# Attention probabilities transposed by a matmul with a diagonal that holds their factor

## What is computed

```python
def _masked_softmax(s, mask):
    ...
    p = jnp.where(mask, jnp.exp(s - m), 0.0)
    return p / jnp.maximum(jnp.sum(p, axis=-1, keepdims=True), 1e-30)
...
o_dsa = jnp.einsum('bhqk,bqkd->bqhd', p.astype(vg.dtype), vg)
...
o_nsa = o_cmp * gt[..., 0:1] + o_slc * gt[..., 1:2] + o_win * gt[..., 2:3]
...
p = jax.nn.softmax(s, axis=-1).astype(v.dtype)          # memory attention
o = jnp.einsum('bhqm,bmhd->bqhd', p, v)
```

## Time and profile before

| | |
|---|---|
| profiled execution | 2762.7 us, its span 2760.9 us |
| median of three runs | 2763.45 us |
| PE busy | 2534.0 us (92%) |
| DVE, ACT, POOL busy | 1292.1, 1049.2, 1250.8 us |
| mean granted clock of PE | 0.95 |
| attention of block 2, units2 | about 2034 to 2264 us of the span |
| memory attention | about 2340 to 2379 us |

### The profile page before, as it was taken

One profiled execution on the slowest core, in us unless ns is written; L12 is line 12 of the kernel. 1 busy time (PEld: TensorE's weight loads), 2 busy tenths in 40 slices (PEclk: granted clock), 3 DMA queues, 4 the chain that ended last, 5 costly groups with the idle time before them and its releaser, 6 DMA issues.

```text
span 2760.9 us, 33141 instructions
## 1 busy us (share of the span) xinstructions
PE 2534.0 (92%) x12115; PEld 2020.5 (73%) x12115; DVE 1292.1 (47%) x2515; ACT 1049.2 (38%) x1619; POOL 1250.8 (45%) x1638
## 2 busy tenths in 40 slices
PE   4898989999999999898999999988886899899998
PEld 3686767888888788676788878877654457688887
DVE  7785442453435577534343251344578853622111
ACT  4233663332222433465242222252255564533322
POOL 4243434656656644334565555562232234355554
PEclk9899999999999999999999999998888589999999
DMA  3221222332222322122233222231110002123222
GB/s 129 70 76 55 71 69 73 104 108 99 92 100 90 106 73 74 58 73 69 81 111 110 98 88 97 91 131 66 50 47 1 1 1 69 58 95 99 92 99 84
DMA packets 80145, 218.05 MB, mean 79 GB/s; under 512 B 15728, under 2 KB 25328, under 8 KB 79472
## 3 DMA queue, kind: packets, MB, share of 16 engines
q1 hardware_dynamic: 60912, 200.96, 22.3%
q10 hardware_dynamic: 19072, 14.98, 1.9%
HBM read 207.25 MB, written 2.10 MB: 76 GB/s over the span
## 4 chain that ended last, share of the span: by engine, by line
PE 76%; DVE 18%; ACT 3%; issue 2%; ACTq 1%; DMA 0%; POOL 0%; DVEq 0%
PE psG L864 22%; PE psG L865 22%; PE psG L866 22%; DVE work_m L1712 3%; DVE tmp L1712 2%; PE psO L1038 1%; DVE work_b L1712 1%; DVE b_lo L1712 1%; DVE work_b L2122 1%; PE psO L1104 1%; DVE max L2121 1%; DVE work_m L1933 1%; PE psT L1015 1%; DVE work_b L2006 1%; PE psG L1049 1%
## 5 line engine op out<-in xcount | busy, mean ns | idle before, releaser
L807 POOL TENSOR_TENSOR w_lo<-w_raw,w_hi 128x256 fp32r<-128x256 f32 x1494 | 1167.8, 813 | 1313.5 <-ACT w_hi L1292 1313.3
L864 PE MATMUL psG<-h_hi,w_hi 128*128 128x512 f32 x1880 | 757.8, 403 | 34.6 <-POOL w_lo L807 30.8
L865 PE MATMUL psG<-h_lo,w_hi 128*128 128x512 f32 x1880 | 740.3, 394 | 0.0
L866 PE MATMUL psG<-h_hi,w_lo 128*128 128x512 f32 x1880 | 739.1, 393 | 0.0
L1292 ACT ACTIVATE w_hi<-w_raw 128x1024 fp32r<-128x1024 f32 (+4 forms) x417 | 403.5, 969 | 497.5 <-PE psG L866 481.2
L864 PEld LDWEIGHTS psG<-h_hi,w_hi 128*128 128x128 f32 x1880 | 358.4, 191 | 122.6 <-issue 43.4
L865 PEld LDWEIGHTS psG<-h_lo,w_hi 128*128 128x128 f32 x1880 | 358.7, 191 | 76.3 <-issue 4.5
L866 PEld LDWEIGHTS psG<-h_hi,w_lo 128*128 128x128 f32 x1880 | 357.9, 190 | 76.8
L864 PE MATMUL psG<-m_hi,w_hi 128*128 128x512 f32 x800 | 311.6, 389 | 1.5 <-DVE m_lo L1712 1.5
L866 PE MATMUL psG<-m_hi,w_lo 128*128 128x512 f32 x800 | 311.2, 389 | 0.0
L865 PE MATMUL psG<-m_lo,w_hi 128*128 128x512 f32 x800 | 311.2, 389 | 0.0
(11 more groups left out here) (284 smaller groups left out, 2940.2 us busy)
## 6 DMA issues: line engine op xcount, KB each, us to landing
w_raw<-wstream SPq DMA_DIRECT2D x327, 512.0 KB, 3.3
w_raw<-wstream SPq DMA_DIRECT2D x64, 256.0 KB, 2.6
w_raw<-wstream SPq DMA_DIRECT2D x16, 384.0 KB, 3.0
work_b<-work_b ACTq DMA_DIRECT2D x16, 256.0 KB, 3.8
work_b<-cmpw ACTq DMA_DIRECT2D x2, 2048.0 KB, 7.7
x<-xT SPq DMA_DIRECT2D x4, 512.0 KB, 6.2
small_work<-ssmp ACTq DMA_DIRECT2D x8, 256.0 KB, 4.1
outT<-x SPq DMA_DIRECT2D x1, 2048.0 KB, 6.3
```

The source lines that it names most:

```text
L807: ins = pool.tensor_tensor(lo[:, c], w[:, c], hi[:, c].bitcast(F32), ALU.subtract)
L864: pe.matmul(out, whi, hi, start=(k == 0), stop=False)
L865: pe.matmul(out, whi, lo, start=False, stop=False)
L866: ins = pe.matmul(out, wlo, hi, start=False, stop=(k == K - 1))
```

## The change

Scaling p is left out. Instead the 128x128 identity is multiplied by the same factor of each row into a new buffer, a diagonal matrix for each a (`factors`, four buffers in turn), by POOL for `units2` and by DVE for x. The blocks of p are turned by an ordinary fp32 matmul with p as the stationary operand and that diagonal as the moving one, in place of a transpose with the identity. POOL and DVE get a wait for the transposes of four units earlier, whose diagonal they overwrite. sw units keep scaling and transpose.

```diff
+        def factors(u):
+
+            return work(R2, 11264 + 256 * (u["n"] % 4), [P, 2, P])
...
             def scale_probs(u):
 
                 n = u["n"]
-                p, _ = probs(u)
-                st = stats(u)
+                st, diag = stats(u), factors(u)
                 pool.wait_ge(s_norm, n - units2[0]["n"] + 1)
+                if n - units2[0]["n"] >= 4:
+                    pool.wait_ge(s_tr, n - 3)
...
-                    ins = pool.tensor_scalar(p[:, a], p[:, a], st[:, 8 + a:9 + a], gate, ALU.mult, ALU.mult)
+                    ins = pool.tensor_scalar(diag[:, a], ident, st[:, 8 + a:9 + a], gate, ALU.mult, ALU.mult)
...
                     for i, m in key_blocks(u):
-                        ins = pe.transpose(out[0:m, a, i * P:(i + 1) * P], p[:, a, i * P:i * P + m], ident)
+                        o, block = out[0:m, a, i * P:(i + 1) * P], p[:, a, i * P:i * P + m]
+                        if u["kind"] == "sw":
+                            ins = pe.transpose(o, block, ident)
+                        else:
+                            ins = pe.matmul(o, block, factors(u)[:, a], start=True, stop=True)
...
-                    ts(p[:, 0], p[:, 0], st[:, 8:9], None, ALU.mult)
-                    ts(p[:, 1], p[:, 1], st[:, 9:10], None, ALU.mult, None, s_prob)
+                    if kind == "x" and n - units["x"][0]["n"] >= 4:
+                        dve.wait_ge(s_tr, n - 3)
+                    out, src = (factors(u), (ident, ident)) if kind == "x" else (p, (p[:, 0], p[:, 1]))
+                    ts(out[:, 0], src[0], st[:, 8:9], None, ALU.mult)
+                    ts(out[:, 1], src[1], st[:, 9:10], None, ALU.mult, None, s_prob)
```

## The result

The changed kernel takes 2773.89 us, the median of five runs (2771.54 to 2780.25); the kernel before took 2763.45 us in five runs beside it (2760.20 to 2767.26). The ratio is 1.0036, 95% interval 1.0024 to 1.0049: slower by some 10 us. The forecast was 2780, with a range of 2764 to 2789. The profiled execution of the changed kernel took 2772.92 us with a span of 2771.1 us.

What follows compares the result with a forecast made beforehand. PE was taken to bound several attention stretches, DVE or ACT the others. Stretch terms summed to +19.6 us, less 3 for the clock, +16.6 on 2762.7, 2779.3 us, stated as 2780; range 2764 to 2789.

Steps and rivals of the forecast that it cites:

- The price of a block: PE, each turned block: a second instruction costing what the first costs, 0.11 us at the full clock, 0.22 at the half.
- 2041 to 2061: First NSA units beside the indexer, PE without pause: 26 more block instructions, +3.4 us.
- The rival of four transposes: All turned blocks: each costs four times a transpose, total about 2832 us; chance 3%.
- 2106 to 2120: Stretch taken as PE without pause: 16 blocks at the full clock, less 0.3 us of pauses, +1.5 us.
- 2152 to 2174: PE without pause at the half clock: 16 blocks, +3.5 us; a clock rise over half the stretch gives 3 back.
- the first rival: Full clock returns in both PE-bound stretches, -10.5 and -8 us, total 2764.6, no measurable difference; chance 14%.
- 2203 to 2223: Narrow NSA units of b = 0, PE without pause: 18 blocks at 0.22 us, nothing hides them, +4.0 us.
- DSA: DSA units, two halves of 42 blocks each: +4.0 us where PE leads, +2.7 where ACT leads and covers part.
- The stretches that DVE leads: Where DVE's selection covers PE: 112 blocks, some 15 us on PE, of which +1.0 us is seen.
- the rival in which it fails: DVE-led stretches: the selection no longer covers PE, half of 15 us is seen, total 2789.5; chance 13%.
- POOL and its new wait: POOL: shorter instructions give nothing more, and the new wait for earlier transposes costs nothing.
- Memory attention: After units2: shorter DVE scalings -1.0 us, bounds -1.5, transposes ahead of a value product +0.5; together -0.5 us.

Runs made afterwards that it cites:

- e5_b1_only: Kernel before, with the change only for the twelve NSA units of query block b = 1: 2766.55 us against 2767.02, ratio 0.9996.
- e2_twice: Kernel before, with each transpose of units2 and memory attention issued twice, scaling of p kept: 2766.74 us, ratio 1.0017.
- e1_null: Kernel before run again without any edit, to see the scatter of profiles: 2767.02 us in one run, beside 2765.22 us in 29 runs.
- e7_fill_b12: Kernel before, plus one unused 512-column fp32 matmul in each unit of b = 2 and b = 1 without an indexer head: 2765.73 us, ratio 0.9994.
- e10_change_b210: Kernel before, with the change only for the NSA units of query blocks b = 2, 1 and 0: 2761.47 us against 2765.35, ratio 0.9987.
- e4_no_dsa: The change without the DSA units, which keep scaling on POOL and the transpose: 2766.10 us, ratio 1.0007 to the kernel before.
- e3_memory_only: Kernel before, with the change for memory attention alone: 2764.56 us, ratio 1.0000.
- e9_twice_nsa: Kernel before, with transposes of the NSA units of all four query blocks issued twice, the others once: 2766.94 us, ratio 1.0002.
- e11_twice_b210: Kernel before, with the transposes of the NSA units of b = 2, 1 and 0 issued twice: 2762.19 us, ratio 0.9988.

## Why the prediction was right, and where not

The direction and the mechanism were right: one more instruction for each of 304 blocks, paid where PE leads. Point by point:

- **The price of a block**, 0.11 us at the full clock: right. Measured (2.05 - 1.09) / 8 = 0.12 us, and 608 instructions of 275 ns. At the half clock e5_b1_only shows +3.3 us for units 24 to 28, where the working had +3.5. The rival of four transposes is out.
- **2041 to 2061**, +3.4 us: measured +3.0, in e2_twice too.
- **2106 to 2120**, +1.5 us: measured -1.1. The working took 0.3 us of pauses where the earlier trace rows show 1.76 (12.24 busy of 14), so it misread a stretch with room as one without. The added work went into the pauses: PE was busy for 15.33 of 18.20 us in units 12 to 16 before and for 16.40 of 17.10 after. The clock rose too (0.91 to 1.00), and this group moved by -0.7 us without any change (e1_null); no run separates the three.
- **2152 to 2174**, +3.5 and -3 for the clock: the rise that was thought likely came, but for the whole of the four units, not for half of them, and it is worth 7.9 us. It is the largest miss of the sum, 5 us. The step that failed is "half of the stretch at the full clock": the clock was already full as unit 24 began and stayed so, and what raised it was work in b = 2 (e7_fill_b12, e10_change_b210), not that of the stretch itself (e5_b1_only). For this stretch the first rival came true, with a smaller gain than its price: 15 us in place of 22 would have been 7 us less than before, and it is 4.6.
- **2203 to 2223**, +4.0 us: measured +3.8 in the change and in e4_no_dsa. The first rival wanted a full clock here too; it was 0.52. That it stayed low was assumed, not derived: e2_twice, with as many instructions, was 8.1 us shorter here. The clock of the change's other executions (0.956 to 0.957) gives no sign that they differ from the profiled one.
- **DSA**, +4.0 and +2.7, together 6.7 us: measured 7.3, of which e4_no_dsa shows 6.6 to be the diagonal's. Right, in size and in the reason: PE leads to the end of the DSA units (busy for 23.63 of the last 25.00 us), and the second half (+3.2) costs a little more than thought. The working has no term for what follows: behind DSA the change gains 2.5 us on e4_no_dsa (column 63-64).
- **The stretches that DVE leads**, +1.0 us: 0.3 - 0.9 + 0.2, nothing that can be told from the scatter. The cover held; the rival in which it fails is out.
- **POOL and its new wait**, nothing: right. The profile puts one pause of POOL, 2.9 us before 2237.84, down to L1024. But the diagonal to be overwritten there was that of unit 46, turned from 2228.3 on, long before; what ended just ahead of 2237.84 is the reciprocal of its own unit (L2037, 2237.58 for 0.17 us). The unit was turned at 2239.57, so it held nobody up.
- **Memory attention**, -0.5 us: measured -2.5, and +2.2 behind it. The net, -0.3, is about what was said, but by luck, for a reason that the working didn't have: the clock was 1.00 there in place of 0.75, and fell just behind. e3_memory_only shows both by itself, and a time unchanged. Up to 1.0 us of the 2.5 is scatter (e1_null).

The working added 16.6 us. By the table 6.6 us were paid from unit 0 to the end, and by the ratio 10 us. Units 24 to 28 (-4.6 for +0.5) and 12 to 16 (-1.1 for +1.5) are 7.7 us of the 10 us between the working and the table, the end of DSA and the products behind it 1.1 (the column 63-64), and DVE's stretches 1.4. The first, 5.1 us, is the clock by e5_b1_only, and most of why the forecast was 6 us too high: the clock's term was sized for half of one stretch. In units 12 to 16 and behind DSA the clock was higher too (0.91 to 1.00, 0.94 to 0.96), but no run takes it out there.

What stays open: what decides the clock of units 37 to 46 (0.52, 0.86, 0.59, 0.53 and 0.54 in five kernels, two of which give PE the same instructions), why e2_twice had a higher mean clock than the change in most of its executions, so whether the kind of instruction has a part in that, and whether the fall behind memory attention is tied to a full clock within it. It stood so in the change, e3_memory_only, e4_no_dsa and e2_twice; but e7_fill_b12 and e9_twice_nsa lost over 4 us there with the code of memory attention unchanged, and e11_twice_b210 nothing.

## What to carry to other kernels

Folding a factor into a transposition by a matmul with a diagonal saves work on the engine that scaled, and costs PE an fp32 matmul's second instruction for each block: do it only where PE has pauses in the same stretch, and not where PE is next to lead, as in DSA here. Cost it by stretch, and give the clock an account of its own, with a term for the whole of a stretch and not for half (7.9 us of 21.9 here), since work added in one stretch can raise the clock of the next. Before a change of the clock is put down to an edit, look at two executions of the kernel without it. A gain from the clock in one part isn't a gain in the time until the runs show it: in e3, e7, e9 and e10 the rest of the kernel was 2.3 to 4.2 us longer.

## What the runs showed of the hardware

- With doubled transposes the clock rose in units 24 to 28 as with matmuls (e2_twice and the change, 1.00 in place of 0.50, -4.6 us in both), and so it did with matmuls that computed nothing, in units ahead of them (e7_fill_b12, -5.1 us). Once, with doubled transposes in e11_twice_b210, it did not (0.66).
- A higher clock did not always buy time: units 24 to 28 of the same kernel took 18.6 us at 0.50 and 18.5 us at 0.66 (before, e1_null).
- More PE work made the next stretch shorter: sixteen fp32 matmul instructions added to units 16 to 24 cost nothing there (-0.8 us, within the scatter), and the next four units were 5.1 us shorter; 4.1 us of it went again behind memory attention (e7_fill_b12).
- The same instructions had the clock at 0.86 in one kernel's execution and at 0.59 in another's (e2_twice, e9_twice_nsa), worth 5 us. Executions of one program spread over 6 us (e4_no_dsa) to 18.6 us (e2_twice, 2760.65 to 2779.26), the longer ones at a lower mean clock (e2_twice: 0.959 and less over 2771 us, 0.960 and more under 2768).
- The lengths of single groups of units repeat to 0.1 us between kernels whose clock runs the same there (the change and e4_no_dsa up to unit 46, the kernel before and e5_b1_only but for units 24 to 28). Where two profiles of this kernel differ by more, the clock is the first thing to compare.
